# Three attentions of a two-block transformer kernel: each head's output is multiplied by spread inverse sums, and probabilities are turned one step on instead of two

## The reference

```python
logits = jnp.where(causal, logits, NEG_INF)
p = jax.nn.softmax(logits, axis=-1).astype(v.dtype)
outs.append(jnp.einsum('bhqk,bhkd->bhqd', p, vb))
...
s = jnp.concatenate([s_loc.reshape(B, H, GRID_W, kr * kc), s_ctx], axis=-1)
p = jax.nn.softmax(s.astype(jnp.float32), axis=-1).astype(q.dtype)
...
s = jnp.einsum('btkgd,bskd->bkgts', q, k)
p = jax.nn.softmax(s.astype(jnp.float32), axis=-1).astype(q.dtype)
return jnp.einsum('bkgts,bskd->btkgd', p, v)
```

## Time and profile before

| | |
|---|---|
| three timed runs | 3159.27, 3156.28 and 8593.32 us; median 3159.27 |
| profiled execution | 3148.98 us, of which the span of the core's instructions is 3147.2 |
| mean granted PE clock | 0.899 of full |
| busy in the span | PE 2537.4 us (81%), DVE 2244.9 (71%), ACT 1557.2 (49%), POOL 332.3 (11%) |
| stage A | about 309 to 384 us of the span |
| stages B and C | about 1312 to 1430 and 1436 to 1550 us |

### The profile page before, as it was taken

How to read it: one execution, slowest core, us unless ns; L and a number is a source line. 1 busy time by engine, 2 the same in 40 slices (tenths; PEclk the granted TensorE clock), 3 DMA queues, 4 the chain that set the end, 5 groups by cost and what they waited for, 6 DMA issues and landing times. The chain is left out here.

```text
span 3147.2 us, 37782 instructions
## 1 busy us (share of the span) xinstructions
PE 2537.4 (81%) x12807; PEld 2077.7 (66%) x12807; DVE 2244.9 (71%) x2177; ACT 1557.2 (49%) x1451; POOL 332.3 (11%) x277
## 2 busy tenths in 40 slices
PE   2959763699981799487784499999999999999991
PEld 2852653577770699376674377777777787777771
DVE  5547755588875211587744589999999999999985
ACT  2213610477661322355521167776666777776660
POOL 1120100123220000000000001111120110111110
PEclk8979885899995899698986599999999999999995
DMA  5745211899972322000211399999999999999984
GB/s 200 264 142 202 48 47 42 292 373 369 359 287 85 127 82 78 29 1 27 81 54 56 122 324 367 366 361 364 364 370 371 366 367 366 366 362 365 363 340 153
DMA packets 254858, 731.70 MB, mean 232 GB/s; under 512 B 29773, under 2 KB 69932, under 8 KB 252528
## 3 DMA queue, kind: packets, MB, share of 16 engines
q1 hardware_dynamic: 228180, 645.62, 56.7%
q0 software_dynamic: 21984, 80.77, 6.8%
q10 hardware_dynamic: 4608, 4.20, 0.4%
HBM read 692.73 MB, written 39.39 MB: 233 GB/s over the span
## 5 line engine op out<-in xcount | busy, mean ns | idle before, releaser
L48 PE MATMUL psum_all<-sb_ring_r,sb_arena_r 128*128 128x512 f32 (+1 forms) x2912 | 1067.3, 367 | 0.0
L152 DVE TENSOR_TENSOR sb_ring_r<-sb_ring,sb_hi_ring 128x2048 fp32r<-128x2048 f32 x297 | 674.4, 2287 | 249.3 <-ACT sb_hi_ring L143 243.6
L47 PE MATMUL psum_all<-sb_hi_ring,sb_arena_r 128*128 128x512 f32 (+1 forms) x1880 | 662.4, 352 | 50.9 <-DVE sb_ring_r L152 47.0
L49 PE MATMUL psum_all<-sb_hi_ring,sb_arena_r 128*128 128x512 f32 (+1 forms) x1880 | 658.1, 350 | 0.0
L143 ACT ACTIVATE sb_hi_ring<-sb_ring 128x2048 fp32r<-128x2048 f32 x297 | 563.7, 1912 | 105.3 <-DMA sb_ring<-in_w_dn_dram 31.5
L48 PEld LDWEIGHTS psum_all<-sb_ring_r,sb_arena_r 128*128 128x128 f32 x2912 | 555.6, 191 | 90.9
L152 DVE TENSOR_TENSOR sb_ring_r<-sb_ring,sb_arena_r 128x2048 fp32r<-128x2048 f32 x258 | 581.3, 2283 | 27.8 <-ACT sb_arena_r L143 27.6
L143 ACT ACTIVATE sb_arena_r<-sb_ring 128x2048 fp32r<-128x2048 f32 x258 | 484.5, 1910 | 199.7 <-DMA sb_ring<-in_w_gu_dram 192.3
L47 PEld LDWEIGHTS psum_all<-sb_hi_ring,sb_arena_r 128*128 128x128 f32 x1880 | 359.2, 191 | 107.3 <-DVE sb_ring_r L152 47.4
L47 PE MATMUL psum_all<-sb_arena_r 128*128 128x512 f32 x1032 | 417.8, 405 | 12.2 <-DVE sb_ring_r L152 7.4
L49 PE MATMUL psum_all<-sb_arena_r 128*128 128x512 f32 x1032 | 408.4, 396 | 0.0
(11 more groups left out here) (369 smaller groups left out, 3212.6 us busy)
## 6 DMA issues: line engine op xcount, KB each, us to landing
sb_ring<-in_w_gu_dram SPq DMA_DIRECT2D x272, 1024.0 KB, 6.7
sb_ring<-in_w_dn_dram SPq DMA_DIRECT2D x136, 1024.0 KB, 8.9
sb_ring<-in_w_e_gate_dram SPq DMA_DIRECT2D x36, 1024.0 KB, 7.6
sb_ring<-in_w_e_up_dram SPq DMA_DIRECT2D x36, 1024.0 KB, 7.1
sb_ring<-in_w_e_down_dram SPq DMA_DIRECT2D x36, 1024.0 KB, 7.9
sb_ring<-in_w_in_dram SPq DMA_DIRECT2D x27, 1024.0 KB, 5.3
sb_arena<-in_w_ada_dram POOLq DMA_DIRECT2D x16, 1024.0 KB, 5.7
sb_ring<-in_w_mod_dram SPq DMA_DIRECT2D x16, 1024.0 KB, 4.8
```

The source lines that it names most:

```text
L47: eng.matmul(out, a[0], b[0], start=start, stop=False)
L48: eng.matmul(out, a[0], b[1], start=False, stop=False)
L49: return eng.matmul(out, a[1], b[0], start=False, stop=stop)
L152: dve.tensor_tensor(s.lo[c % SLOTS], s.raw[c % SLOTS], s.hi[c % len(s.hi)].bitcast(F32), ALU.subtract).then_inc(s.lo_made, 1)
```

## The change

The probabilities are no longer scaled. They stay exponentials, are turned by PE as soon as their exp is done, one step after it instead of two, and so rounded and split one step on; the products with the values begin one step earlier. `scale` is gone from DVE. `inverse` gets eight columns.

In step `4h + 5`, PE spreads the four inverse columns of head `h` over a bank: four f32 matmuls of 128x128, whose weights are one column of `inverse` repeated 128 times and whose moving operand is the identity, so that each row of the result holds the 512 inverses. The bank is one of the two of the turned probabilities (`kept` lists such turns). ACT copies the head's 64 rows of it to `spec.factors`, right behind the exp and ahead of the late groups and the query's split. In step `4h + 7` DVE multiplies the head's 64x512 product in PSUM by them (`make_whole`): in A straight into the output, in B and C into `spec.whole`, out of which ACT makes the upper and DVE the lower half, both in step `4h + 8`; before, the upper half was made in step `4h + 8` and the lower in `4h + 9`. `factors` and `whole` lie in `k.neg_sel`, whose contents A has copied before. The line numbers of the changed kernel are 14 to 40 higher in and after this function.

```diff
     def mixing(u):
-        if u < 4 or u > NU + 3:
+        if u < 3 or u > NU + 2:
             return None
-        return (u - 4) // 2, (u - 4) % 2
+        return (u - 3) // 2, (u - 3) % 2
 
     def leaving(u):
+        return (u - 7) // TILES if u >= 7 and (u - 7) % TILES == 0 and u < NU + 4 else None
+
+    def spreading(u):
+        return (u - 5) // TILES if u >= 5 and (u - 5) % TILES == 0 and u < NU + 5 else None
+
+    at, m, kept = {}, len(first), []
     for u in range(STEPS):
-        if 2 <= u <= NU + 1:
-            for i in range(len(parts(u - 2))):
-                at["p", u - 2, i] = m
+        if 1 <= u <= NU:
+        if spreading(u) is not None:
+            at["s", spreading(u)] = m
+            kept.append(m)
+            m += 1
...
         def _(pe):
+            def bank_free(m):
+                if m - 2 in kept:
+                    pe.wait_ge(s.copied, kept.index(m - 2) + 1)
+                elif m >= 2:
+                    pe.wait_ge(s.split, halved(m - 2))
...
             def turn_probs(u):
-                pe.wait_ge(s.scaled, u + 1)
+                pe.wait_ge(s.exp_done, u + 1)
...
                     if pair % 2 == 0 and h >= 2:
-                        pe.wait_ge(s.out_hi, h - 1)
-                        if spec.splits:
-                            pe.wait_ge(s.out_lo, h - 1)
+                        pe.wait_ge(s.whole, h - 1)
...
+            def spread(h):
+                m = at["s", h]
+                bank_free(m)
+                pe.wait_ge(s.inverted, TILES * (h + 1))
+                for t in range(TILES):
+                    column = inverse[:, (TILES * h + t) % 8]
+                    ins = pe.matmul(k.psum[:, 4 + m % 2, t * P:(t + 1) * P], wide(column, 1, P), k.ident[:],
+                                    start=True, stop=True)
+                ins.then_inc(s.turned, 1)
             for u in range(STEPS):
                 if u < NU:
                     score(u)
-                if 2 <= u <= NU + 1:
-                    turn_probs(u - 2)
+                if 1 <= u <= NU:
+                    turn_probs(u - 1)
                 if mixing(u) is not None:
                     mix(*mixing(u))
+                if spreading(u) is not None:
+                    spread(spreading(u))
                 for i, group in enumerate(spec.late.get(u, ())):
                     fill(at["l", u, i], group["src"])
...
             for u in range(STEPS):
-                if 2 <= u <= NU + 1:
-                    v = u - 2
+                if 1 <= u <= NU:
+                    v = u - 1
                     if v >= 4 and v % 2 == 0:
                         act.wait_ge(s.mixed, v - 2)
...
                 if u < NU:
                     exp(u)
+                if spreading(u) is not None:
+                    h = spreading(u)
+                    m, rows = at["s", h], spec.out(h)[2]
+                    act.wait_ge(s.turned, m + 1)
+                    if h >= 2:
+                        act.wait_ge(s.whole, h - 1)
+                    act.activation(spec.factors[rows], k.psum[rows, 4 + m % 2, :], ACT.Copy).then_inc(s.copied, 1)
                 for i, group in enumerate(spec.late.get(u, ())):
                     if group["after"]:
                         act.wait_ge(s.scored, group["after"])
                     rounded(at["l", u, i], group["hi"], bank(at["l", u, i], group["hi"].shape[-1]))
                 hooks.act_step(act, u, s)
-                if leaving(u) is not None:
-                    h = leaving(u)
-                    act.wait_ge(s.mixed, 4 * h + 4)
-                    dst, rows = spec.out(h)[0], spec.out(h)[2]
-                    act.activation(dst, k.psum[rows, 6 + h % 2, :], ACT.Copy).then_inc(s.out_hi, 1)
+                if spec.splits and leaving(u - 1) is not None:
+                    h = leaving(u - 1)
+                    dst, _, rows = spec.out(h)
+                    act.wait_ge(s.whole, h + 1)
+                    act.activation(dst, spec.whole[rows], ACT.Copy).then_inc(s.out_hi, 1)
...
             def invert(u):
                 dve.wait_ge(s.exp_done, u + 1)
-                if u >= 4:
-                    dve.wait_ge(s.scaled, u - 3)
-                dve.reciprocal(inverse[:, u % 4:u % 4 + 1], total[:, u % 4:u % 4 + 1]).then_inc(s.inverted, 1)
-
-            def scale(u):
-                part = probs[u % 3][:, 0:spec.n(u % TILES)]
-                dve.wait_ge(s.inverted, u + 1)
-                dve.tensor_scalar(part, part, inverse[:, u % 4:u % 4 + 1], None, ALU.mult).then_inc(s.scaled, 1)
+                if u >= 8:
+                    dve.wait_ge(s.copied, u // TILES - 1)
+                dve.reciprocal(inverse[:, u % 8:u % 8 + 1], total[:, u % 4:u % 4 + 1]).then_inc(s.inverted, 1)
+
+            def make_whole(h):
+                dst, _, rows = spec.out(h)
+                dve.wait_ge(s.copied, h + 1)
+                dve.wait_ge(s.mixed, 4 * h + 4)
+                if spec.splits and h >= 2:
+                    dve.wait_ge(s.out_lo, h - 1)
+                dve.tensor_tensor(spec.whole[rows] if spec.splits else dst, k.psum[rows, 6 + h % 2, :],
+                                  spec.factors[rows], ALU.mult).then_inc(s.whole, 1)
...
                 if 1 <= u <= NU:
                     invert(u - 1)
-                    scale(u - 1)
-                if 2 <= u <= NU + 1:
-                    v = u - 2
+                if 1 <= u <= NU:
+                    v = u - 1
...
                 hooks.dve_step(dve, u, s)
+                if leaving(u) is not None:
+                    make_whole(leaving(u))
                 if spec.splits and leaving(u - 1) is not None:
                     h = leaving(u - 1)
                     out_hi, out_lo, rows = spec.out(h)
                     dve.wait_ge(s.out_hi, h + 1)
-                    dve.tensor_tensor(out_lo, k.psum[rows, 6 + h % 2, :], out_hi.bitcast(F32), ALU.subtract).then_inc(s.out_lo, 1)
+                    dve.tensor_tensor(out_lo, spec.whole[rows], out_hi.bitcast(F32), ALU.subtract).then_inc(s.out_lo, 1)
...
+    spec.whole, spec.factors = (k.neg_sel[:, i:i + 4, :].rearrange("p h n -> p (h n)") for i in (0, 4))
```

More of the change, by code:

```diff
@@ L900, in attend @@
     NU = HEADS * TILES
-    STEPS = NU + 6
+    STEPS = NU + 5
     hi, lo = turned
@@ L924, in attend, with halved @@
             m += 1
+    def halved(m):
+        return m + 1 - sum(x <= m for x in kept)
     needed = {}
@@ L927, in attend @@
         for i, group in enumerate(groups):
-            needed[group["by"]] = max(needed.get(group["by"], 0), at["l", u, i] + 1)
+            needed[group["by"]] = max(needed.get(group["by"], 0), halved(at["l", u, i]))
     logits = k.psum[:, 0:4, :].rearrange("p (b a) n -> p b (a n)", b=2)
     with stage(nc) as ctx:
-        s = sems(nc, ctx, name, "scored", "biased", "max_ready", "exp_done", "inverted", "scaled", "turned", "rounded",
-                 "split", "mixed", "out_hi", "out_lo")
+        s = sems(nc, ctx, name, "scored", "biased", "max_ready", "exp_done", "inverted", "turned", "rounded", "split",
+                 "mixed", "copied", "whole", "out_hi", "out_lo")
         hooks = make(nc, ctx)
-        neg_max, total, inverse = k.small[:, 0:2], k.small[:, 8:12], k.small[:, 16:20]
+        neg_max, total, inverse = k.small[:, 0:2], k.small[:, 8:12], k.small[:, 16:24]
         block = ctx.enter_context(nc.Block())
@@ L981, in mix @@
                 if half == 0:
-                    pe.wait_ge(s.split, at["p", last, len(parts(last)) - 1] + 1)
+                    pe.wait_ge(s.split, halved(at["p", last, len(parts(last)) - 1]))
                     if pair == 0:
```

9 lines of the change are left out of this document (4 added, 5 removed).

## The result

Sixteen runs of each kernel: before 3150.03 us median, changed 3162.93; ratio 1.0046, 95% interval 1.0035 to 1.0057, so 11 to 18 us slower, well within the two per cent. The profiled execution took 3158.56 us (span 3156.8) against 3148.98 (3147.2). The time lies 1 us from the 3164 on record, by luck: the difference forecast was +5 and the measured one 13, and the median of three from which I started lay 9 us above that of sixteen; the two errors cancel. Of the difference, the sign was forecast and the size was not.

The account below looks back on a forecast made before the run. No engine was full, so the bound was read from the time between exps on ACT. A's heads +6.3, A's start -1, B +0.7 and C's tail -1 gave +5 on the 3159.27 median: 3164 us, range 3148 to 3184.

Parts of the forecast that it names:

- The loops: Exp, turning, rounding, next exp: plain steps 1.15 to 2.0 us in A, 2.0 and 2.4 in B, 2.5 in C.
- The head of A: First attention, four steps per head: 8.3 us against 7.24, +1.05; over six heads +6.3 us.
- the split step: Step with a query's split in A: next exp after 3.36 us instead of 2.28, delayed by spread and copy.
- the spread: Four added f32 matmuls on PE per head: 0.45 us, doubled to 0.9 as upper bound.
- the prediction's own +6 for 13 heads: Bound on the sum: a spread of 0.9 us would add 0.45 to each of 13 heads, +6 us.
- The head of C: Third attention: 3.3, 4.2, 2.7 and 2.5 us, together 12.7 against 12.76, so 0.
- the third rival: A bank or split holds early turning back a step: old loops plus additions, within 5 us; chance 0.05 with the unforeseen.
- B held: Second attention: a head of 12.75 us against 12.32, +2.7 for six heads; with the tail's -2, +0.7 us.
- the first chain: On ACT and DVE in B: exp, output's upper half, lower half, bias, maximum, next exp: 3.54 us; 3.3 in C.
- A's start: A scale of 4.01 us beside a POOL operation goes: -1 us taken, between -3.9 and 0.
- The first (DVE's relief is passed on): Rival: DVE is the bound; B gives -10 us, C -3, A +1 or unchanged: 3147 us; chance 0.2.
- The second (PE's clock falls): Rival: PE waits each step and its clock drops, +12 us over eleven heads of A and C: 3176 us; chance 0.25.

Follow-up runs that it names:

- experiment 1: Changed kernel with the factors' copy on ACT moved behind the late groups and the query's split: 3154.24 us, ratio 1.0022 to the kernel before.
- experiment 4: Changed kernel with the four spread matmuls made twice over the same bank: 3181.32 us, ratio 1.0105 to the kernel before.
- experiment 3: Changed kernel with turning, rounding, splitting and value products put back to the old lag of two steps: 3143.06 us, ratio 0.9983 to the kernel before.
- Experiment 9: Changed kernel with DVE's lower half of the output one step behind ACT's upper half: 3166.32 us, ratio 1.0039 to the kernel before.
- experiment 8: Kernel before, scaling kept, but turned, rounded and split one step on, without spread or factors: 3368.17 us, ratio 1.0703 to the kernel before.
- experiment 5: Changed kernel with the old lag of two steps and the factors' copy behind the query's split: 3148.36 us, ratio 0.9997 to the kernel before.

## Why the prediction held, and what was off

**Direction and cause held.** Slower by less than a per cent, most of it in A, in the step with the query's split, by the spread on PE and the copy on ACT (experiments 1 and 4). The relief of DVE was not passed on. The size of the difference did not hold: +5 put, +13 measured, and that 3164 came out is luck. What the prediction has nowhere is the price of the lag. It wrote down the loop that early turning closes and found the steps without a query's split together as long as before; that the same kernel with the old lag has shorter ones, by about 20 us in all, only experiment 3 showed.

**The loops held.** A's plain steps were put at 1.8, 2.0 and 1.15 us; they took 1.76, 2.01 and 1.19 (2.07 in every other head, where a key is split as well, which I had left out). B's were put at 2.4 and 2.7 and took 2.34 and 2.56, and 2.65 and 2.81 in the other kind of head.

**The head of A was mis-sized:** 8.3 us put, 9.02 measured. Of the 0.7 that lack, the smaller part is the split step: 3.36 put, 4.18 and 3.06 in turn, so 3.62 in the mean. The larger is the step in which a key is split, 1.15 put and 1.19 and 2.07 in turn, 1.63 in the mean. The kernel before has it too (1.45 and 2.11), so its 7.24 holds a key's split and the 8.3 set against it does not.

In the split step the term that was off is the spread, 0.45 put, at most 0.9, measured 1.05. The row that I took the price from the earlier trace rows counts 16 instructions, and the loop that issues them makes eight matmuls (`for kd in range(KD)`, with `KD` = 1024 / 128), so each f32 matmul stood there as two instructions, as in the spread, and cost 0.23 and not 0.11. I had divided by instructions and not by calls; four would have been 0.92, which is what four more did cost (0.90, experiment 4), the copy would have come 1.5 us after the exp (measured 1.59 in the long steps, 0.72 in the others), and by the prediction's own +6 for 13 heads the sum would have been +11, the lower end of what was measured. That it gets so near is again partly luck, since it leaves out the key's split. The row of six transposes was misread as well: 0.85 / 6 is 0.14 and not 0.11. From rows of this case such a matmul costs about twice a transpose (0.26 against 0.14). The Trainium skill's factor of four (TensorE: Matmul & The Clock Gate, section Terms) gave 1.8 us for the spread, 0.75 too much, where 0.45 was 0.6 too little.

**The head of C was mis-sized too:** 12.7 put, 13.23 measured, since the split step was put at 4.2 and took 4.84, with the wait for the bank (0.81) in it that I had named under the third rival and not priced. B held: 12.75 put, 12.86 measured over two heads at the full clock. Experiment 9 shows that the first chain (3.54 put, 3.65 and 3.38 measured) was real, but that removing it shifts the time to the next step.

**A's start** gave nothing back, where -1 was put. Timeline of DVE and POOL, answering to the earlier trace rows:

```profile
310.64 5.40 POOL L1272 TENSOR_TENSOR sb_arena<-sb_arena 2x2048 f32<-2x2048 f32 x1
...
313.58 3.55 DVE L1300 TENSOR_TENSOR sb_ring_r<-sb_arena,sb_ring_r 128x1024 fp32r<-128x1024 f32 x1 [1.32 <-ACT sb_ring_r L1296]
```

The subtraction of the values now spans the end of POOL's operation. From the first exp to the third stand 11.7 us after and 11.8 before. The trace has the same subtraction three times under a POOL operation, at 313.29 before and at 308.97 and 313.58 after; it takes 2.67, 2.69 and 3.55 us and each time ends 1.08 or 1.09 us after POOL's operation. Begun between two of them, at 320.33 before, it takes 1.21. That is what the Trainium skill, SBUF — State Buffer, section SBUF: two separate sides, would have: an instruction of DVE that reads two operands from SBUF waits for the whole of a POOL operation that reads it, so the lock falls on the subtraction when the scale is gone. Not all that the trace has fits this: the query's subtraction of 64x512 behind it, begun at 317.15 under a POOL operation of 3.64 us from 316.13, takes 1.41 us, twice its usual 0.69, but does not wait for that operation's end.

**The rivals.** The first (DVE's relief is passed on) did not happen, but experiment 3 shows that some of it was there to be had, in B alone, and that the shorter lag consumed it. The second (PE's clock falls) did not happen; experiment 8 shows a kernel in which the clock is low. The third was partly there, as C's wait for the bank.

## What to carry to other kernels

Taking work off the busiest engine and shortening a pipeline's lag in one edit can cancel: here the first was worth about 5 us and the second cost about 20, and only the run that separates them shows it. A lag of one step puts every engine's hand-over into one loop, so first write that loop down through each engine's queue, with what stands ahead in it. An added operation is priced by where it stands: half a us of copy or one of matmul costs nothing, itself, or itself and a bank's wait, by what is queued behind it, and moved out of one long step it often comes back in the next.

## What the runs showed of the hardware

- An f32 matmul of 128x128 on 128 columns that is no transpose appears as two instructions, and four took 1.05 us with their weights, eight 1.95, so 0.23 each. With one column instead of 128 the price is the same (eight in 1.84 us). Six transposes of the same size took 0.85.
- A DVE subtraction of 128x1024 with both operands in SBUF took 1.21 us between two POOL operations and 2.67 to 3.55 when begun under one, and ended 1.08 or 1.09 us after it.
- The granted clock is no property of a stage: in A it averaged 0.84 before, 0.92 after, and 0.58 with the lag alone, PE being busy 78, 79 and 63% of the stretch. In B it fell to the half level in the middle of the stage in some profiles (before, changed) and not in others (experiments 1, 3, 4 and 5), and cost an estimated 0.5 to 1.4 us each time.
